# The first modulation by chunks of channels, folded and used chunk by chunk

## The chip, the cores and the metric

The kernel runs on one core of one Trainium2 chip. The metric is the device time of one execution in microseconds (us), as the median of the runs.

## The reference, cut to what matters

Two layers of a first block (two mixers, each with a feed-forward part) and two layers of a second block (attention over a memory, a mixture of experts at the end) act on 256 tokens of `x` and 256 tokens of a context, 1024 channels each. What the change touches is the beginning of layer 0:

```python
mod = silu(c) @ ada_w[0] + ada_b[0]        # 6 x 1024 values; the same with c_ctx for the context
shift, scale = mod[0:1024], mod[1024:2048]  # of the mixer; the other four parts are used later
h  = rmsnorm(x, norm_mix_w[0]) * (1.0 + scale) + shift
hc = rmsnorm(ctx, norm_mix_w[0]) * (1.0 + scale_ctx) + shift_ctx
p  = h @ ab_w_in[0]                         # 1024 -> 2560 columns; hc likewise
```

Apart from this, and at the same time in the kernel, stand the keys and values of the memory of layer 0 (`mem @ xa_w_k`, `mem @ xa_w_v`), which do not depend on `x`.

## The kernel before, in words

Everything is transposed: a tensor of 512 tokens (256 of `x`, side 0; 256 of the context, side 1) lies as 8 chunks of 128 channels on the partitions, with the tokens in the free dimension. Weights come as one long stream of slots of 1 MB (16 tiles of 128x128 f32) through a ring of six slots (`ring`). SyncE issues the loads in order. A load of slot n waits until TensorE has begun slot n-5 (the semaphore `slots_used`). GpSimd's queue issues the other loads.

Large products are done in three: a weight slot is split into a rounded high part (ScalarE, `slot_high_act`, L986) and the rest (VectorE, `slot_low_dve`, L994), the input likewise, and TensorE adds high x high, high x low and low x high in a bank of PSUM. A slot's low part overwrites the slot in the ring. The order of each engine's work is written out by hand; engines meet only through semaphores.

The start of the kernel runs like this on TensorE (L1899 to L1952):

- filler matmuls, then two column groups of the memory's keys with slot K0a, in plain f32
- the first modulation, 2048 columns (`ada_products`, L1909): eight slots A0 to A7, one for each 128 rows of `ada_w`. The weights of the array are the two columns of `silu(c)`, the slot is streamed, and four column groups of the array write 512 columns each, to partitions 0-1, 32-33, 64-65, 96-97 of one bank. Sums over all 1024 rows, so no value is known before A7.
- between them the other keys (K0b), the sums of squares of the norm (L572), the values (V0a, V0b, `mem_value_products`, L1845 to L1849) and the spread of 1/rms over the partitions (L605)
- `turn_rows` (L1937): ScalarE and VectorE copy the four rows of 512 to `ada_row`, TensorE turns them with 16 small matmuls into 16 columns of 128 channels, VectorE adds the bias (L3023) and makes the scale of all 8 chunks (L2968)
- `split_products` (L1182) of the input, `ab_w_in`, slots AB0 and AB1: a pair of output tiles chunk by chunk (L1158 to L1164) as VectorE scales (`rms_split_dve`, L1073), ScalarE shifts and rounds (L1060), and VectorE makes the low part (L1080); then two more output tiles (L1176 to L1180)
- `split_token_products` with AB2 and AB3 (L1222 to L1226), and so on.

VectorE's own order behind the modulation is (L3030 to L3037): the low part of AB0, all chunks of the input, the low part of AB1, then for n = 2 to 6 three chunks of the later modulation (`first_chunks`, L2988, two passes of 128x1024 each) and the low part of slot AB n. The later modulation's chunks wait for the two rows of `silu(c)`, which ScalarE makes from a load (`silu_rows`, L2616); GpSimd issues that load when TensorE has begun AB0 (L3681).

The load order was: memory, K0a, A0, A1, K0b, `x`, `ctx`, A2, A3, V0a, A4, A5, V0b, A6, A7, AB0, AB1, and on.

Of the kernel before, what the change touches and what calls it, by code (L numbers as in the profile page):

```python
# [9 lines left out]
F32 = mybir.dt.float32  # L10
# [3 lines left out]
ALU = mybir.AluOpType  # L14
# [30 lines left out]
    ("ident", P), ("ones", P), ("eps", 2), ("final_norm_w", DC), ("ln_g", 6 * DC), ("ln_b", 6 * DC), ("ckv_gain", 1), ("decay_b", 4), ("head_norm_w", 1),  # L45
# [5 lines left out]
    ("slot_id", P), ("earlier", P), ("fold", 32),  # L51
# [14 lines left out]
SLOTS_ADA = 16 * DC // TILES  # L66
# [10 lines left out]
START = ["K0a", "A0", "A1", "K0b", "A2", "A3", "V0a", "A4", "A5", "V0b", "A6", "A7"]  # L77
# [35 lines left out]
def build(nc, stream, ada_stream, mem_w, c_rows, small, x_t, ctx_t, mem_t, ab_bias, sgu, t5_bias, band_bias, cmp_bias, out):  # L113
    with ExitStack() as ctx:
# [22 lines left out]
        silu_c = sb("silu_c", 2 * DC)  # L137
# [50 lines left out]
        ada_row = area(0, 2048)  # L188
# [1618 lines left out]
        def _(pe):  # L1807
# [98 lines left out]
            sums, ada_bank = bk.next_bank(), bk.next_bank()  # L1906
            rows_out = bk.freed(bk.turn - 1)

            def ada_products(k):  # L1909
                rows, first = w.tiles(TILES)  # L1910
                for j in range(4):
                    m = nc.tensor.matmul(PS[ada_bank][32 * j:32 * j + 2, :], silu_c[:, 2 * k:2 * k + 2],
                                         rows[:, j * 512:(j + 1) * 512], start=k == 0, stop=k == DC - 1)
                    if first and j == 0:
                        m.then_inc(sem("slots_used"), 1)
                if k == DC - 1:
                    m.then_inc(full(ada_bank), 1)

            for k in range(2):
                ada_products(k)  # L1920
            pe.wait_ge(sem("mem_split"), DC)
            mem_key_products(range(2, 4))
            ada_products(2)
# [4 lines left out]
            ada_products(3)  # L1928
            mem_value_products()
            rstd_pe(bk, TT)  # L1930
            for k in range(4, 6):
                ada_products(k)
            mem_value_products()
            for k in range(6, DC):
                ada_products(k)

            def turn_rows():  # L1937
                b = bk.next_bank()
                pe.wait_ge(*rows_out)
                pe.wait_ge(sem("rows_copied"), 1)  # L1940
                for n in range(TILES):
                    columns, rows = PS[b][:, 2 * n:2 * n + 2], ada_row[0:2, n * P:(n + 1) * P]
                    if n == 0:
                        nc.tensor.matmul(columns, rows, ident[0:2, 0:2], start=True, stop=True)
                    else:
                        m = nc.tensor.transpose(columns, rows, ident[0:2, 0:2])
                m.then_inc(full(b), 1)

            turn_rows()
            split_products(bk, w, 4, ab_high, h_part, TT, ab_slot_high, sides=2)  # L1950
# [630 lines left out]
        def _(act):  # L2581
# [14 lines left out]
            nc.scalar.activation(silu_c[:, :], small_at("c2"), ACT.Silu).then_inc(sem("silu_c_ready"), 1)  # L2596
# [3 lines left out]
            slot_high_act(bk, START.index("K0b"), mem_slot_high, fresh=True)  # L2600
# [3 lines left out]
            for name in ("V0a", "V0b"):  # L2604
                slot_high_act(bk, START.index(name), mem_slot_high, fresh=True)
            b = bk.next_bank()
            act.wait_ge(full(b), bk.filled())
            for j in range(2):
                m = nc.scalar.activation(ada_row[0:2, j * 512:(j + 1) * 512], PS[b][32 * j:32 * j + 2, :], ACT.Copy)
            m.then_inc(free(b), 1)  # L2610
            bk.turn += 2
            last = bk.freed(bk.turn - 2)
            for n in range(4):
                bk.fill(MEM_BANKS[n % 2])

# [4 lines left out]
            slot_high_act(bk, AB_AT, ab_slot_high, fresh=True)  # L2620
            slot_high_act(bk, AB_AT + 1, ab_slot_high, fresh=True)
            act.wait_ge(sem("mod_ready"), 1)
            shift_high_act(bk, 0, 0, 2, ab_high, last)
            for t in range(2):
                b = bk.fill(MEM_BANKS[t])
                act.wait_ge(full(b), bk.filled())
                nc.scalar.activation(mem_made_values(t), PS[b][:, :], ACT.Copy).then_inc(free(b), 1)
# [45 lines left out]
            act.wait_ge(sem("mod_ready"), 2)  # L2673
# [17 lines left out]
            act.wait_ge(sem("mod_ready"), 4)  # L2691
# [262 lines left out]
        def _(dve):  # L2954
# [10 lines left out]
            def mod_scaled(l, m, sides=2):  # L2965
                nw = small_at(("norm_mix_w", "norm_ffn_w")[m], "p (l c s) -> p l c s", l=2, c=DC)
                at = slice(24 * m + 8, 24 * m + 16)
                nc.vector.scalar_tensor_tensor(scalev[:, l, m, :, 0:sides], modv[:, l, at, 0:sides], 1.0,  # L2968
                                               nw[:, l, :, 0:sides], ALU.add, ALU.mult).then_inc(sem("mod_ready"), 1)
                dve.wait_ge(sem("mod_ready"), 2 * l + m + 1)  # L2970
# [39 lines left out]
            for c in range(1, 4):  # L3010
                mem_key_out(c)
            root_dve(bk, TT)
            for name in ("V0a", "V0b"):
                slot_low_dve(bk, START.index(name), mem_slot_high)
            b = bk.next_bank()
            dve.wait_ge(full(b), bk.filled())
            for j in range(2, 4):
                ins = nc.vector.tensor_copy(ada_row[0:2, j * 512:(j + 1) * 512], PS[b][32 * j:32 * j + 2, :])
            ins.then_inc(sem("rows_copied"), 1)
            spread = spread_dve(bk)  # L3020
            b = bk.next_bank()
            dve.wait_ge(full(b), bk.filled())
            nc.vector.tensor_tensor(mod[:, 0:32], PS[b][:, 0:32], ada_b[:, 0:32], ALU.add).then_inc(free(b), 1)  # L3023
            dve.wait_ge(*bk.freed(bk.turn - 1))
            for b in MEM_BANKS:
                bk.fill(b)
            marks["mem_out"] = [bk.freed(bk.turn - n) for n in (2, 1)]
            mod_scaled(0, 0)
            dve.wait_ge(sem("x_landed"), 32)
            slot_low_dve(bk, AB_AT, ab_slot_high)  # L3030
            rms_split_dve(bk, 0, 0, 2, ab_high, spread=spread)
            slot_low_dve(bk, AB_AT + 1, ab_slot_high)
# [644 lines left out]
        def _(pool):  # L3677
            pool.dma_start(consts[:, 0:N_EARLY], small[:, 0:N_EARLY]).then_inc(sem("small_landed"), 16)
            nc.gpsimd.memset(filler[:, :], 1.0).then_inc(sem("filler_set"), 1)
# [89 lines left out]
        def _(sp):  # L3769
# [12 lines left out]
            for n in range(4):  # L3782
# [3 lines left out]
            for n in range(4, RING):  # L3786
                load(n)
            before = N_SLOTS - SLOTS_MOE
            groups = before // RING
            with nc.sync.Fori(0, groups - 1) as i:  # L3790
                for n in range(RING, 2 * RING):
                    load(n, i, RING, at=n + i * RING)
# [145 lines left out]
def _layout(i):  # L3938
# [12 lines left out]
    slots_of("A", _by_row(i["ada_w"][0][:, 0:2048]), "01234567")  # L3951
# [64 lines left out]
    arrays = [stream.reshape(N_SLOTS, P, SLOT), ada, mem_w, c_rows, _small(i), turned(i["x"][0]), turned(i["ctx"][0]),  # L4016
# [21 lines left out]
```

## Time and profile before

| what | us |
|---|---|
| median of 3 runs (2561.82 to 2563.05) | 2561.86 |
| profiled execution, whole | 2562.03 |
| its span | 2560.2 |
| TensorE busy | 2497.3 (98%) |
| VectorE busy | 1988.4 (78%) |
| ScalarE busy | 1175.9 (46%) |

The profile is one execution. Times in its rows are counted from the start of the span. In the names of engines PE is TensorE (PEld its weight loads), DVE VectorE, ACT ScalarE, POOL GpSimd, SP SyncE. An f32 matmul stands as two records, one of rounded values as one.

### The profile page before, as it was taken

How to read it: one execution, taken by the hardware profiler on the slowest of the kernel's cores; microseconds unless marked ns; L12 is line 12 of the kernel's file. 1: busy time of each engine (PE TensorE's matmuls, PEld its weight loads, DVE VectorE, ACT ScalarE, POOL GpSimd, SP SyncE). 2: the span in 40 equal slices, each digit the busy share in tenths (PEclk: the TensorE clock that was granted, in tenths of full speed). 3: DMA queues.
4: the chain of work that ended last, by engine and by line, in shares of the span. 5: the costliest groups of instructions: out<-in, count | busy, mean ns of one | idle time of the engine just before them, and what ended most of it. 6: DMA issues, size and time to landing. Idle time of an engine off the chain costs nothing.

```text
span 2560.2 us, 42423 instructions
## 1 busy us (share of the span) xinstructions
PE 2497.3 (98%) x16691; PEld 2147.3 (84%) x16691; DVE 1988.4 (78%) x2455; ACT 1175.9 (46%) x1498; POOL 89.1 (3%) x116
## 2 busy tenths in 40 slices
PE   7999999999999999999999899999999999999998
PEld 5877788888889998889999688888888888888886
DVE  3886877777766886857887748888888888988887
ACT  3435200001421004531014736777777777777776
POOL 0100100000000001000002000000000000000000
PEclk8999999999999999999999999999999999999999
DMA  8843444443335553334555035999899989999996
GB/s 333 315 166 130 168 171 166 168 167 116 116 108 212 186 182 137 111 108 159 185 182 185 15 116 194 373 363 375 334 374 366 363 343 374 366 351 358 362 375 247
DMA packets 91399, 602.77 MB, mean 235 GB/s; under 512 B 9840, under 2 KB 12912, under 8 KB 24688
## 3 DMA queue, kind: packets, MB, share of 16 engines
q1 hardware_dynamic: 76848, 540.05, 55.9%
q0 software_dynamic: 14400, 60.56, 6.7%
q8 instruction: 113, 1.85, 0.3%
q14 instruction: 38, 0.31, 0.0%
HBM read 598.47 MB, written 2.10 MB: 235 GB/s over the span
## 4 chain that ended last, share of the span: by engine, by line
PE 92%; DVE 5%; ACT 2%; issue 1%; DMA 1%; SPq 0%; DVEq 0%; ACTq 0%
PE bank L1176 12%; PE bank L1179 12%; PE bank L1180 12%; PE bank L2477 8%; PE bank L2481 8%; PE bank L2480 8%; PE bank L2508 4%; PE bank L2512 4%; PE bank L2511 4%; PE bank L532 2%; PE bank L1413 1%; PE bank L1434 1%; ACT arena L1458 1%; PE bank L2490 1%; PE bank L572 1%; PE bank L1226 1%
## 5 line engine op out<-in xcount | busy, mean ns | idle before, releaser
L972 DVE TENSOR_TENSOR ring_part<-ring,arena_part 128x2048 fp32r<-128x2048 f32 x481 | 1079.3, 2274 | 29.0 <-ACT arena_part L991 14.6
L2833 ACT ACTIVATE arena_part<-ring 128x2048 fp32r<-128x2048 f32 x339 | 647.6, 1920 | 192.9 <-DMA ring<-in_stream 192.4
L1176 PE MATMUL bank<-arena_part 128*128 128x256 f32 (+1 forms) x2040 | 651.5, 319 | 8.1 <-DVE ring_part L972 8.1
L1180 PE MATMUL bank<-arena_part,ring_part 128*128 128x256 f32 (+1 forms) x2040 | 648.0, 318 | 0.0
L1179 PE MATMUL bank<-h_part,arena_part 128*128 128x256 f32 (+1 forms) x1496 | 474.9, 317 | 0.0
L1176 PEld LDWEIGHTS bank<-arena_part 128*128 128x128 f32 x2040 | 389.9, 191 | 38.7 <-issue 12.4
L1180 PEld LDWEIGHTS bank<-arena_part,ring_part 128*128 128x128 f32 x2040 | 389.9, 191 | 25.7
L2477 PE MATMUL bank<-arena_part,h_part 128*128 128x512 f32 x896 | 354.2, 395 | 0.0
L2481 PE MATMUL bank<-arena_part,h_part 128*128 128x512 f32 x896 | 349.6, 390 | 0.0
L2480 PE MATMUL bank<-ring_part,h_part 128*128 128x512 f32 x896 | 348.9, 389 | 0.0
L1280 ACT ACTIVATE arena<-bank 128x256 f32<-128x256 f32 (+1 forms) x66 | 30.1, 456 | 636.6 <-PE bank L1180 635.6
L1179 PEld LDWEIGHTS bank<-h_part,arena_part 128*128 128x128 f32 x1496 | 285.7, 191 | 18.6
L968 DVE CAST arena_part<-ring 128x2048 fp32r<-128x2048 f32 x115 | 140.5, 1222 | 74.9 <-PE bank L1176 71.0
L2481 PEld LDWEIGHTS bank<-arena_part,h_part 128*128 128x128 f32 x896 | 168.1, 188 | 36.2
L2480 PEld LDWEIGHTS bank<-ring_part,h_part 128*128 128x128 f32 x896 | 168.4, 188 | 33.6
L2477 PEld LDWEIGHTS bank<-arena_part,h_part 128*128 128x128 f32 x896 | 168.3, 188 | 33.2
L2508 PE MATMUL bank<-arena_part 128*128 128x512 f32 x448 | 175.2, 391 | 0.0
L2512 PE MATMUL bank<-arena_part 128*128 128x512 f32 x448 | 174.4, 389 | 0.0
L2511 PE MATMUL bank<-ring_part,arena_part 128*128 128x512 f32 x448 | 174.4, 389 | 0.0
L1179 PE MATMUL bank<-arena_part 128*128 128x256 f32 (+1 forms) x544 | 173.2, 318 | 0.0
L972 DVE TENSOR_TENSOR arena_part<-bank,arena_part 128x512 fp32r<-128x512 f32 x56 | 38.7, 691 | 94.9 <-ACT arena_part L2918 94.9
L1179 PEld LDWEIGHTS bank<-arena_part 128*128 128x128 f32 x544 | 104.3, 192 | 6.8
(376 smaller groups left out, 3087.8 us busy)
## 6 DMA issues: line engine op xcount, KB each, us to landing
ring<-in_stream SPq DMA_DIRECT2D x511, 1024.0 KB, 4.9
arena<-in_ada_stream POOLq DMA_DIRECT2D x80, 512.0 KB, 4.3
consts<-in_mem_w POOLq DMA_DIRECT2D x8, 512.0 KB, 4.0
consts<-in_small POOLq DMA_DIRECT2D x1, 2800.0 KB, 11.6
arena<-in_c_rows POOLq DMA_DIRECT2D x2, 1024.0 KB, 7.6
arena<-in_ab_bias POOLq DMA_DIRECT2D x1, 2048.0 KB, 8.8
arena<-in_t_bias POOLq DMA_DIRECT2D x1, 2048.0 KB, 9.0
arena<-in_mem_t SPq DMA_DIRECT2D x1, 1024.0 KB, 4.9
```

The lines of the kernel that those rows point to most:

```text
L968: nc.vector.tensor_copy(high, value).then_inc(sem("rounded"), 1)
L972: return nc.vector.tensor_tensor(low, value, high.bitcast(F32), ALU.subtract)
L1176: m = nc.tensor.matmul(out_ap, w_high, high, start=start, stop=False)
L1179: nc.tensor.matmul(out_ap, w_high, low, start=False, stop=False)
L1180: return nc.tensor.matmul(out_ap, w_low, high, start=False, stop=stop)
L2477: m = nc.tensor.matmul(PS[b][:, :], x_e_high[:, k, of(e)], high, start=k == 0, stop=False)
L2480: nc.tensor.matmul(PS[b][:, :], x_e_high[:, k, of(e)], low, start=False, stop=False)
L2481: m = nc.tensor.matmul(PS[b][:, :], x_e_low[:, k, of(e)], high, start=False, stop=k == DC - 1)
L2508: m = nc.tensor.matmul(PS[b][:, :], h_high, high, start=f_blk == 0 and f == 0, stop=False)
L2511: nc.tensor.matmul(PS[b][:, :], h_high, low, start=False, stop=False)
L2512: m = nc.tensor.matmul(PS[b][:, :], h_low, high, start=False, stop=f_blk == MB - 1 and f == FB - 1)
L2833: nc.scalar.activation(high, ring[:, where], ACT.Copy).then_inc(sem("moe_high"), 1)
```

## The change

- The weights of the first modulation leave the stream and become a tensor of their own, `ada_mix`: eight pieces of 1 MB, piece c holding all 1024 rows of the 128 shift columns and the 128 scale columns of channel chunk c. They are loaded into the first four rooms of the ring, behind AB1, and the stream goes on behind them.
- `silu_c` becomes eight blocks of 32 columns, two of `silu` and 30 of zero (cleared by GpSimd). For a chunk, column group g takes the rows k = g and then k = 4 + g: eight f32 matmuls of 256 columns, into 4 x 32 partitions of one bank. ScalarE copies the bank to `ada_rows`.
- `fold_rows`: two f32 matmuls with 128x128 of `ada_rows` as weights and the first two columns of `fold` (1 where the partition modulo 32 is the column) sum the four groups and turn the rows. VectorE adds the bias and makes the scale of that chunk alone.
- `first_products`: the products of chunk k with four output tiles at once (slots AB0 and AB1), 12 matmuls of 512 columns, where there were two tiles and then two.
- The loop: products of piece c+2, fold of c+1, products of the input with chunk c.
- Moved: the values of the memory stand earlier and together; the copies of the values out of PSUM, on ScalarE both before, are one on ScalarE and one on VectorE and stand ahead of the modulation; V0b is split by VectorE alone; AB0 and AB1 are split ahead of the modulation.

```diff
-START = ["K0a", "A0", "A1", "K0b", "A2", "A3", "V0a", "A4", "A5", "V0b", "A6", "A7"]
+START = ["K0a", "K0b", "V0a", "V0b"]
@@ tensor
             pe.wait_ge(sem("mem_split"), DC)
             mem_key_products(range(2, 4))
-            ada_products(2)
+            mem_value_products()
+            sums = bk.next_bank()
             for c in range(DC):
                 pe.wait_ge(sem("squared"), bk.up("squared"))
                 m = group_sums(sums, sqv[:, c, :], TT, c == 0, c == DC - 1)
             m.then_inc(full(sums), 1)
-            ada_products(3)
             mem_value_products()
+            marks["values_full"] = [(full(b), bk.filled_in[b]) for b in MEM_BANKS]
             rstd_pe(bk, TT)
...
+            def ada_products(c):
+                b = bk.fill(ADA_BANKS[c % 2])
+                rows_copied.append(bk.freed(bk.turn - 1))
+                pe.wait_ge(free(b), bk.emptied())
+                pe.wait_ge(sem(f"ada_landed{c % ADA_ROOMS}"), 16 * (c // ADA_ROOMS + 1))
+                room = ring[:, c % ADA_ROOMS * SLOT:(c % ADA_ROOMS + 1) * SLOT]
+                for late in range(2):
+                    for g in range(4):
+                        k = 4 * late + g
+                        m = nc.tensor.matmul(PS[b][32 * g:32 * g + 32, X2], silu_c[:, k, :],
+                                             room[:, k * SEQ:(k + 1) * SEQ], start=not late, stop=bool(late))
                 m.then_inc(full(b), 1)
+                ada_made.append((full(b), bk.filled()))
+
+            def fold_rows(c):
+                pe.wait_ge(*rows_copied[c])
+                b = bk.fill(FOLD_BANK)
+                pe.wait_ge(free(b), bk.emptied())
+                for n in range(2):
+                    m = nc.tensor.matmul(PS[b][:, 4 * c + 2 * n:4 * c + 2 * n + 2], ada_rows[c % 4][:, n * P:(n + 1) * P],
+                                         small_at("fold")[:, 0:2], start=True, stop=True)
+                m.then_inc(full(b), 1)
...
+            ada_products(0)
+            ada_products(1)
+            fold_rows(0)
+            for c in range(DC):
+                if c + 2 < DC:
+                    ada_products(c + 2)
+                if c + 1 < DC:
+                    fold_rows(c + 1)
+                first_products(c)
+            w.t += 2 * TILES
@@ scalar
+            copy_rows(0)
+            copy_rows(1)
+            for c in range(DC):
+                if c + 2 < DC:
+                    copy_rows(c + 2)
+                for s in range(2):
+                    t = slice(SEQ * s, SEQ * (s + 1))
+                    scaled_act(bk, c == DC - 1 and s == 1, spread_last)
+                    nc.scalar.activation(ab_high[:, c, t], hv[:, c, t], ACT.Identity, bias=shift(0, 0, c, s))\
+                        .then_inc(sem("in_high"), 1)
@@ vector
+            for c in range(DC + 1):
+                if c < DC:
+                    b = bk.fill(FOLD_BANK)
+                    dve.wait_ge(full(b), bk.filled())
+                    both = modv[:, 0, c:c + DC + 1:DC, :]
+                    nc.vector.tensor_tensor(both, PS[b][:, 4 * c:4 * c + 4].rearrange("p (n s) -> p n s", n=2),
...
+                    nc.vector.scalar_tensor_tensor(scalev[:, 0, 0, c, :], modv[:, 0, DC + c, :], 1.0, mod_w[:, 0, c, :],
+                                                   ALU.add, ALU.mult).then_inc(sem("dve_step"), 1)
+                    dve.wait_ge(sem("dve_step"), bk.up("dve_step"))
+                    for s in range(2):
+                        t = slice(SEQ * s, SEQ * (s + 1))
+                        ins = nc.vector.scalar_tensor_tensor(hv[:, c, t], xv[:, c, t], scalev[:, 0, 0, c, s:s + 1],
+                                                             PS[spread][:, t], ALU.mult, ALU.mult)
+                        scaled_dve(ins, c == DC - 1 and s == 1, spread)
+                if c:
+                    for s in range(2):
+                        t = slice(SEQ * s, SEQ * (s + 1))
+                        dve.wait_ge(sem("in_high"), bk.up("in_high"))
+                        ins = nc.vector.scalar_tensor_tensor(h_part[:, c - 1, t], hv[:, c - 1, t], shift(0, 0, c - 1, s),
+                                                             ab_high[:, c - 1, t].bitcast(F32), ALU.add, ALU.subtract)
+                    ins.then_inc(sem("in_split"), 1)
             bk.turn += 4 + 4
             dve.wait_ge(sem("c_rows_ready"), 1)
@@ sync
+            for j in range(DC):
+                if j >= ADA_ROOMS:
+                    sp.wait_ge(*marks["ada_made"][j - ADA_ROOMS])
+                elif j == ADA_ROOMS - 1:
+                    for made in marks["values_full"]:
+                        sp.wait_ge(*made)
+                else:
+                    sp.wait_ge(sem("slots_used"), j + 2)
+                room = ring[:, j % ADA_ROOMS * SLOT:(j % ADA_ROOMS + 1) * SLOT]
+                sp.dma_start(room, ada_mix[j, :, :]).then_inc(sem(f"ada_landed{j % ADA_ROOMS}"), 16)
```

The new load order is: memory, K0a, K0b, `x`, `ctx`, V0a, V0b, AB0, AB1, the eight pieces, AB2, and on.

## Rows read from the trace of the kernel before

**Rows 1.** The page's busy times: us, share of the span, instructions.
```profile
PE 2497.3 (98%) x16691; PEld 2147.3 (84%) x16691; DVE 1988.4 (78%) x2455; ACT 1175.9 (46%) x1498; POOL 89.1 (3%) x116
```

**Rows 2.** The chain of waits, 0 to 260: start us, us, what.
```profile
30.08 1.79 PE bank L572 x64
...
57.12 0.94 PE bank L1946 x15
58.59 2.29 DVE ring_part L972
...
71.90 1.34 DVE h_part L1080 x4
...
75.83 0.47 PE bank L1176
```

**Rows 3.** Windows: stretch, length; busy us and records of each engine; clock, DMA share, GB/s.
```profile
125.00:130.00 5.00, 5.00 (x24) 4.14 (x23) 4.96 (x8) 0.60 (x1) 1.05 (x2) 1.00 0.58 202
```

**Rows 4.** Timeline of TensorE: start us, us, engine, line, what.
```profile
86.81 0.39 PE L1222 MATMUL bank<-arena_part 128*128 128x512 f32 x1
...
141.20 0.39 PE L1176 MATMUL bank<-arena_part 128*128 128x512 f32 x1
141.43 0.39 PE L1179 MATMUL bank<-h_part,arena_part 128*128 128x512 f32 x1
```

**Rows 5.** Timeline of VectorE, 69 to 140; in brackets the idle time before.
```profile
69.46 0.86 DVE L1073 SCALAR_TENSOR_TENSOR h_normed<-x_stream,mod_scale,bank 128x256 f32<-128x256 f32 x2
70.25 0.87 DVE L1080 SCALAR_TENSOR_TENSOR h_part<-h_normed,mod,arena_part 128x256 fp32r<-128x256 f32 x2
...
76.83 1.23 DVE L2983 SCALAR_TENSOR_TENSOR arena<-arena 128x1024 f32<-128x1024 f32 x1 [1.14 <-ACT arena L2618]
...
83.71 2.29 DVE L972 TENSOR_TENSOR ring_part<-ring,arena_part 128x2048 fp32r<-128x2048 f32 x1
...
138.00 2.28 DVE L972 TENSOR_TENSOR ring_part<-ring,arena_part 128x2048 fp32r<-128x2048 f32 x1
```

**Rows 6.** Timeline of all engines, 0 to 40.
```profile
10.01 7.14 PE L1824 MATMUL bank<-arena,ring 128*128 128x256 f32 x32
...
17.08 1.90 PE L1912 MATMUL bank<-ring,silu_c 128*2 128x512 f32 x16
17.39 1.91 ACT L991 ACTIVATE arena_part<-ring 128x2048 fp32r<-128x2048 f32 x1 [4.88 <-DMA ring<-in_stream]
...
22.73 0.20 ACT L637 ACTIVATE stats<-consts 128x1 f32<-128x1 f32 x1 [2.13 <-DMA x_stream<-in_ctx_t]
...
36.53 0.77 PE L1845 MATMUL bank<-arena_part 128*128 128x512 f32 x1 [3.84 <-DVE ring_part L972]
```

**Rows 7.** The page's groups: count, busy us, mean ns of one, idle before.
```profile
L1280 ACT ACTIVATE arena<-bank 128x256 f32<-128x256 f32 (+1 forms) x66 | 30.1, 456 | 636.6 <-PE bank L1180 635.6
...
L968 DVE CAST arena_part<-ring 128x2048 fp32r<-128x2048 f32 x115 | 140.5, 1222 | 74.9 <-PE bank L1176 71.0
```

**Rows 8.** Timeline of ScalarE, 69 to 77.
```profile
69.97 0.91 ACT L1060 ACTIVATE arena_part<-h_normed,mod 128x256 fp32r<-128x256 f32 x2 [0.67 <-DVE h_normed L1073]
...
73.59 1.28 ACT L2618 ACT_TABLE_LOAD   x1
74.88 1.92 ACT L2618 ACTIVATE arena<-arena 128x2048 f32<-128x2048 f32 x1
```

**Rows 9.** The page's loads: queue, count, KB each, median us to landing.
```profile
ring<-in_stream SPq DMA_DIRECT2D x511, 1024.0 KB, 4.9
```

**Rows 10.** Windows of 0.5 us where TensorE begins again and where its clock rises.
```profile
36.50:37.00 0.50, 0.47 (x1) 0.50 (x2) 0.00 (x0) 0.00 (x0) 0.00 (x0) 0.50 1.03 426
41.50:42.00 0.50, 0.50 (x3) 0.41 (x2) 0.50 (x1) 0.00 (x0) 0.00 (x0) 0.53 0.53 213
62.50:63.00 0.50, 0.46 (x1) 0.49 (x2) 0.50 (x2) 0.50 (x2) 0.00 (x0) 0.50 0.00 0
65.50:66.00 0.50, 0.50 (x3) 0.37 (x3) 0.50 (x3) 0.50 (x2) 0.21 (x1) 0.63 1.02 426
```

More of the change, by code:

```diff
@@ L50 @@
     ("sinks", 8), ("expert_id", EXPERTS), ("cmp_row_ok", 2),
-    ("slot_id", P), ("earlier", P), ("fold", 32),
+    ("slot_id", P), ("earlier", P),
 ]
@@ L110, in leave, with build @@
         self.i = None
-def build(nc, stream, ada_stream, mem_w, c_rows, small, x_t, ctx_t, mem_t, ab_bias, sgu, t5_bias, band_bias, cmp_bias, out):
+def build(nc, stream, ada_mix, ada_stream, mem_w, c_rows, small, x_t, ctx_t, mem_t, ab_bias, sgu, t5_bias, band_bias, cmp_bias, out):
     with ExitStack() as ctx:
@@ L1904, in _ @@
             pe.wait_ge(sem("silu_c_ready"), 1)
[L1906 to L1920, printed above, removed]
             pe.wait_ge(sem("mem_split"), DC)
             mem_key_products(range(2, 4))
-            ada_products(2)
+            mem_value_products()
+            sums = bk.next_bank()
             for c in range(DC):
@@ L2599, in _ @@
                 nc.scalar.activation(mem_high[:, c, :], mem_in[:, c, :], ACT.Copy).then_inc(sem("mem_rounded"), 1)
-            slot_high_act(bk, START.index("K0b"), mem_slot_high, fresh=True)
+            for name in ("K0b", "V0a"):
+                slot_high_act(bk, START.index(name), mem_slot_high, fresh=True)
             act.wait_ge(sem("x_landed"), 32)
@@ L2603, in _, with copy_rows @@
             root_act(bk, TT, 0)
[L2604 to L2612, printed above, removed]
+            for n in range(2):
+                slot_high_act(bk, AB_AT + n, ab_slot_high, fresh=True)
             for n in range(4):
                 bk.fill(MEM_BANKS[n % 2])
+            b = bk.fill(MEM_BANKS[0])
+            act.wait_ge(full(b), bk.filled())
+            nc.scalar.activation(mem_made_values(0), PS[b][:, :], ACT.Copy).then_inc(free(b), 1)
+            bk.fill(MEM_BANKS[1])
+            bk.turn += 1
+            spread_last = bk.freed(bk.turn - 1)
+            def copy_rows(c):
+                b = bk.fill(ADA_BANKS[c % 2])
+                act.wait_ge(full(b), bk.filled())
+                nc.scalar.activation(ada_rows[c % 4], PS[b][:, X2], ACT.Copy).then_inc(free(b), 1)
+            copy_rows(0)
[8 more added lines that the diff above has]
+                        .then_inc(sem("in_high"), 1)
+            for _ in range(DC):
+                bk.fill(FOLD_BANK)
             def silu_rows(rows, times):
@@ L3009, in _ @@
             slot_low_dve(bk, START.index("K0b"), mem_slot_high)
-            for c in range(1, 4):
-                mem_key_out(c)
+            mem_key_out(1)
+            mem_key_out(2)
+            slot_low_dve(bk, START.index("V0a"), mem_slot_high)
+            mem_key_out(3)
+            split_slot(bk, START.index("V0b"), None, highs=mem_slot_high)
             root_dve(bk, TT)
-            for name in ("V0a", "V0b"):
-                slot_low_dve(bk, START.index(name), mem_slot_high)
-            b = bk.next_bank()
+            for n in range(2):
+                slot_low_dve(bk, AB_AT + n, ab_slot_high)
@@ L3789, in _ @@
             groups = before // RING
-            with nc.sync.Fori(0, groups - 1) as i:
-                for n in range(RING, 2 * RING):
+            with nc.sync.Fori(0, groups - 2) as i:
+                for n in range(2 * RING, 3 * RING):
                     load(n, i, RING, at=n + i * RING)
```

112 lines of the change are left out of this document (60 added, 52 removed).

## The prediction

> **What bounds the kernel now.** I read the shares of busy time first: TensorE is busy 98% of the span, the other engines are not near it [rows 1]. So a microsecond counts only where TensorE stands still, and the change touches only the first 90 us. The chain of waits shows the place: TensorE ends the columns of the modulation at 58.06, VectorE spends 2.29 us on the first input slot, then scales and splits chunk after chunk until 73.24 and splits the second slot right behind, and TensorE goes on at 75.83 [rows 2]. From there it has no hole: a stretch of 5 us holds 5.00 us of it [rows 3], and the values' products begin at 86.81 [rows 4]. These need slot AB2 in two parts, and VectorE ends that at 83.71 + 2.29 = 86.00, only 0.8 us earlier, because three chunks of the later modulation stand before it (six passes, from 76.83 on) [rows 5]. The same order, three chunks and then a slot, repeats for later slots: AB7 is split at 138.00 + 2.28 = 140.28 [rows 5] and needed at 141.20 [rows 4]. The reader is to see two queues that run side by side with next to no play: **what counts is not when TensorE gets its first product, but when VectorE is through with the modulation and reaches AB2.** A change that frees TensorE earlier and VectorE later loses.
>
> **Start, up to the first product.** Eight MB of modulation weights leave the front of the load queue. The fifth 1 MB transfer of it landed at 17.4 and the seventh at 22.7 [rows 6], so 2.65 us each. In the new order K0b is third (12.1), V0a sixth (20.0), V0b seventh (22.7), AB0 and AB1 by 28, the modulation's chunks 0 and 1 by 33.4.
> - K0a's products run from 10.01 to 17.15 as before [rows 6]. K0b is split by then, its 48 matmuls of 256 columns, half of the 0.23 us that 512 take [rows 4], run 17.3 to 23.0.
> - V0a: ScalarE 1.91 us [rows 6] from 20.0, VectorE 2.29 us, the fourth key copy some 0.4 us (ScalarE's of that size is 0.46 [rows 7]): TensorE starts 24.8, 24 matmuls at 0.23 us [rows 4] end 30.3.
> - Sums 1.8 us [rows 2]: 32.2. V0b was split by VectorE meanwhile (1.22 [rows 7] and 2.29 us): products 32.3 to 37.8. Spread, half as many records as the sums, 0.9 us: 38.9.
> - Modulation products: 16 records took 1.90 us for 2 MB [rows 6]; a chunk now is 1 MB in eight matmuls of 256 columns, four column groups side by side: 0.95 us. Chunk 0 ends 39.95, chunk 1 41.0.
> - The fold is two f32 matmuls with 128x128 weights and two columns, four records; the trace has none like it. Below: the turns at 0.94/15 = 0.06 us a record [rows 2], 0.25 us. Above: K0a's records at 7.14/32 = 0.22 us [rows 6], 0.9 us. I take 0.45, since two columns stream next to nothing and only the weights count. Fold 0 ends 41.55, chunk 2's products 42.6.
> - ScalarE is in order: it copies chunk c+2's rows before it shifts chunk c. Copy 0.46 us [rows 7], two shifts 0.91 us [rows 8], about 0.1 us for handing over: 1.5 us. **First product of the input at 44.1**, where the kernel now has its first in the half microsecond from 62.50 [rows 10]: 18 us won, and spent in the loop.
>
> The Trainium skill, in "TensorE: Matmul & The Clock Gate", Part 3 (Packing small matmuls), gives 2.38 times for three column tiles side by side. Worked out as an estimate for four, that is 3.17 times and 1.13 us instead of 0.95 for a chunk, 1.1 us more over the six chunks inside the loop, and 2566.4 in the end. The trace disagrees: eight matmuls of 512 columns in 1.90 us are 0.24 us each, against 0.89 us for one alone (twice 7.14/16), so 3.75 times [rows 6].
>
> **The loop.** Per chunk TensorE does 12 matmuls (240 lie between 86.81 and 141.20 [rows 4], 0.227 us each: 2.72 us), 0.95 us for chunk c+2, 0.1 us between. The fold hides beside ScalarE's copy. But products of chunk c wait for both shifts, these wait behind the copy of chunk c+2, and that one waits for products made just before: 1.5 us in which TensorE has only the fold. Period 1.5 + 2.72 + 0.1 + 0.95 = 5.27 us. VectorE needs 0.53 us from the fold's end through bias and scale (58.06 to 58.59 [rows 2]), 0.79 for two scalings (69.46 to 70.25) and as much for two splits [rows 5], 2.1 us: never the limit. Loads: chunk j waits for chunk j-4's products, three periods ahead, against 4.9 us to land [rows 9]: hidden. Chunk 5's products start at 44.1 + 5 x 5.27 = 70.45 and end 73.2; fold 7 ends 73.75. VectorE then has bias and scale, two scalings, split 6 and split 7, 0.53 + 3 x 0.79: **it is through at 76.6**. TensorE, limited by split 6, ends the four tiles at 79.5 (before: 86.8).
>
> **After the loop.** VectorE's next work are the three chunks, which wait for the activated rows. ScalarE ends the last shift at about 75.5; table load 1.28 and the pass 1.92 us [rows 8] make 78.7. The rows themselves are in time: GpSimd issues their load at TensorE's first product of the input, 31 us before. First pass at 78.8, **2.0 us later than 76.83**. The value copies that left ScalarE's queue (1.1 us) are in this already. AB2 is split at 88.0, so TensorE, idle from 79.5, begins the values' products at 88.1: 1.3 us late. The copies and slot splits moved into the start stand beside TensorE's 5.5 us stretches; if they were uncovered they would cost up to 2 us before 44.1, and as much in the end.
>
> **The clock.** After 8.6 us of nothing TensorE starts at the lower level. The trace shows this twice: work began at 36.5 with a granted clock of 0.50, and it stayed there until about 41.6; work began at 62.5 and it stayed until about 65.7 [rows 10]. So 5.1 and 3.2 us at 1.2 GHz instead of 2.4, a loss of 2.6 and 1.6 us. In this kernel the second one fell where VectorE was the limit and cost little; in the new one it falls on the values' products, with TensorE the limit from there. I take 2.1 us. Price with its bounds: 1.6 to 2.6.
>
> Sum: +1.3 + 2.1 = +3.4 us. VectorE is then 2.0 us late and TensorE 3.4, so no later slot is waited for; both keep the distance to the end. The profiled execution took 2562.03 (span 2560.2 and 1.8 around it), which gives 2565.4; it lies 0.2 above the median of the runs, so **2565.3**.
>
> **Rivals.** A measurement of this kernel tells about 0.2%, 5.1 us, from no change.
> - A, the loop is paced by TensorE alone (period 4.3, copy and shift hidden better than I think): five periods of 1.0 us less, VectorE is through at 71.8, products of AB2 start at 83.3, -3.5 + 2.1: 2560.5. For it: the shifts of chunk c could start in the period before. Against: ScalarE's order. 0.22.
> - B, TensorE's lead is kept and values' products start at 79.5: -7.3, 2554.6. Against: six passes at 1.15 us stand between the last split and AB2's, whatever TensorE does. 0.05 for this or anything as large.
> - C, other side: TensorE, with 1.1 us holes in each period and a pause of 1.8 us before V0a, falls to the lower level inside the loop. A period then is 1.5 + 5.4 + 0.1 + 1.9 = 8.9, so 3.6 us more each; one is enough to leave the 0.2% (2568.9), two give 2572.5, seven 2590. For: it was at the lower level at 36.5 after one pause only [rows 10]. Against: that pause was 3.8 us with no work in it (until 36.53 [rows 6]), and 80% of each period is work. 0.08.
> - D, each hand-over costs 0.1 us more than I took (five in a period, seven periods): 3.5 us on the end of VectorE's part, 2568.8. 0.10.
> - The forecast, 2562.5 to 2567: 0.55.
>
> Both ends of the fold's price (it is on the path twice) give -0.4 and +0.9. Range 2559.5 to 2569: it holds the forecast, A and most of D, and leaves out B and C. Faster by over 0.2%: B and a little of A, 0.06. Slower: C and D and the upper end of the forecast, 0.18. The same: 0.76.
>
> **What would show it.** In the timeline: first product of the input near 44 (right if 42 to 47); starts of chunk c's products 5.3 us apart, each after a shift of ScalarE; the first later chunk on VectorE near 79; TensorE idle for 7 to 9 us before the values' products, ended by VectorE's split of AB2; a granted clock of 0.5 in the 3 to 5 us after it. The forecast is wrong if the period is under 4.5 or over 6, if AB2's split ends before 85, or if the clock is at 0.5 between 45 and 79.

## The result and the profile after

The changed kernel takes 2567.16 us (median of 22 runs, 2562.46 to 2569.06). The kernel before takes 2561.86 on the same chip (22 runs, 2559.03 to 2563.83). The ratio is 1.0018, 95% interval [1.0012, 1.0024]: 3.1 to 6.1 us slower, a little on the slow side of "no difference", with the edge of 5.1 us inside the interval. The forecast was 2565.3, in a range up to 2569. The profiled execution of the changed kernel took 2563.34 (span 2561.5), which lies near the fast end of its runs; why, is told below.

The page's busy times answer to [rows 1]:

```profile
PE 2495.5 (97%) x16770; PEld 2146.4 (84%) x16770; DVE 1992.0 (78%) x2469; ACT 1174.0 (46%) x1502; POOL 89.3 (3%) x117
```

Everything that the change does lies in the first 90 us. The chain of waits of the changed kernel, from 0 to 130 (start us, us, what), answers to [rows 2]:

```profile
25.11 0.47 PE bank L1845
...
30.95 1.88 PE bank L572 x64
32.83 0.43 PE bank L1845
...
39.59 1.73 PE bank L1934 x32
41.32 0.54 PE bank L1944 x4
41.86 1.04 PE bank L1934 x16
42.93 0.38 ACT arena L2650
43.31 0.80 ACT arena_part L2660 x2
44.16 0.50 PE bank L1958
46.27 0.91 PE bank L1966 x4
47.17 1.05 PE bank L1934 x16
48.24 0.38 ACT arena L2650
48.62 0.80 ACT arena_part L2660 x2
49.47 0.50 PE bank L1958
...
70.75 0.50 PE bank L1958
...
75.99 1.28 ACT L2667
77.29 1.93 ACT arena L2667
79.24 1.23 DVE arena L3024 x2
...
86.20 2.22 DVE ring_part L972
88.55 0.76 PE bank L1222
```

One turn of the loop can be read off it. TensorE makes a piece's products (L1934), ScalarE copies them (L2650) and only then shifts the chunk of two pieces earlier (L2660), and TensorE's products of the input (L1958) wait for that. From 44.16 to 49.47 is 5.31 us, and it is the same five times, up to 70.75. Then the chain leaves TensorE: ScalarE's table and pass, the three later chunks on VectorE, the split of AB2 (L972), and last the values' products (L1222) at 88.55, where they stood at 86.81 before [rows 4].

The same place in TensorE's timeline (in brackets the idle time before, and what ended it):

```profile
25.11 0.47 PE L1845 MATMUL bank<-arena_part 128*128 128x512 f32 x1 [2.05 <-DVE arena L3043]
...
79.12 1.07 PE L1966 MATMUL bank<-h_part,arena_part 128*128 128x512 f32 x4
88.55 0.76 PE L1222 MATMUL bank<-arena_part 128*128 128x512 f32 x1 [8.36 <-DVE ring_part L972]
89.11 0.63 PE L1225 MATMUL bank<-ring_part,arena_part 128*128 128x512 f32 x1
```

So TensorE is free 6.6 us earlier (80.2 against 86.8), stands still for 8.36 us, and begins 1.74 us later. Then it is slow: starts are 0.43 us apart, where 0.23 is usual [rows 4]. Windows of the changed kernel show the clock (stretch, length, busy us and records of PE, PEld, DVE, ACT, POOL, then PE's granted clock, DMA share, GB/s); the last is for later on:

```profile
82.50:83.00 0.50, 0.00 (x0) 0.00 (x0) 0.50 (x3) 0.50 (x1) 0.00 (x0) 0.77 1.24 524
83.00:83.50 0.50, 0.00 (x0) 0.00 (x0) 0.50 (x1) 0.50 (x2) 0.00 (x0) 0.50 0.70 287
88.50:89.00 0.50, 0.45 (x1) 0.48 (x2) 0.50 (x1) 0.00 (x0) 0.00 (x0) 0.50 0.95 377
92.50:93.00 0.50, 0.50 (x3) 0.37 (x2) 0.50 (x3) 0.00 (x0) 0.00 (x0) 0.50 0.97 410
93.00:93.50 0.50, 0.50 (x4) 0.41 (x3) 0.50 (x1) 0.00 (x0) 0.22 (x1) 0.99 1.00 393
1400.00:1440.00 40.00, 34.31 (x270) 27.26 (x271) 31.81 (x90) 23.52 (x66) 9.16 (x2) 1.00 0.15 55
```

The clock fell to half (1.2 GHz) in the pause and came back at 93.0, after 4.5 us of work. At the full clock that work takes half of this time, so the fall costs 2.2 us.

Where the rest of the kernel stands is read from a mark that both have, ScalarE's table load ahead of the second mixer. In the kernel before, then in the changed one:

```profile
312.94 1.28 ACT L1280 ACT_TABLE_LOAD   x1
```

```profile
317.09 1.28 ACT L1280 ACT_TABLE_LOAD   x1
```

That is 4.15 us, and as much at 617.64 and 621.79: 1.74 + 2.2 and some tenths. But at the end of the kernel the two profiled executions are only 1.3 us apart. Table loads of ScalarE that both have show where they come together. At 1089.51 and 1092.25 they are 2.74 apart. TensorE of the kernel before has a wait shortly ahead of that which the changed one doesn't have:

```profile
1041.39 2.00 PE L1413 MATMUL bank<-arena 64*128 64x256 f32 x16 [1.20 <-ACT arena L2587]
```

All profiles with the new start lack this wait and gain about 1.5 us on before there; b1, which has the old start, has the wait and gains nothing. So it goes with the change, but why is not shown. At 1396.19 and 1399.69 the two are 3.50 apart again, and at 1483.04 and 1484.16 only 1.12. This last step has to do with the clock: from 1400 to 1440 that of the execution before was

```profile
1400.00:1440.00 40.00, 36.22 (x258) 27.29 (x257) 31.82 (x91) 23.53 (x67) 9.16 (x2) 0.87 0.15 53
```

0.87, with a fall to 0.50 from about 1414 to 1424, and the changed kernel's was 1.00. Nothing there was changed, and all the other profiles of this document have a fall at that place. Four of the changed kernel's 22 runs have a mean clock of 0.996 or more, as the profiled one has, and take 2562.5 to 2564.3; the other 18 have 0.993 or 0.994 and take 2564.9 to 2569.1. **The profiled execution is one of the few with a fall less**, so the medians, not the two spans, tell the cost. e10 below is in all but one load the changed kernel, and its profile has the fall at 1414 and one more at the start: its span is 5.7 us above before's (2565.9 against 2560.2), which is near the 5.3 of the medians.

### The profile page after: what moved, and what is told of

It reads as the page before. It is cut to its first block, busy times and chain, and to the rows that moved or that the text cites. A ratio compares the mean times of both kernels' runs of the same rounds, so it can differ in the third digit from the quotient of the medians.

```text
span 2561.5 us, 42582 instructions
## 1 busy us (share of the span) xinstructions
PE 2495.5 (97%) x16770; PEld 2146.4 (84%) x16770; DVE 1992.0 (78%) x2469; ACT 1174.0 (46%) x1502; POOL 89.3 (3%) x117
## 4 chain that ended last, share of the span: by engine, by line
PE 91%; DVE 4%; ACT 2%; issue 1%; DMA 1%; SPq 0%; DVEq 0%; ACTq 0%
PE bank L1176 12%; PE bank L1179 12%; PE bank L1180 12%; PE bank L2506 8%; PE bank L2510 8%; PE bank L2509 8%; PE bank L2537 4%; PE bank L2541 4%; PE bank L2540 4%; PE bank L532 2%; PE bank L1413 1%; PE bank L1434 1%; PE bank L572 1%; ACT arena L1458 1%; PE bank L1222 1%; PE bank L2519 1%
## 5 line engine op out<-in xcount | busy, mean ns | idle before, releaser
L972 DVE TENSOR_TENSOR ring_part<-ring,arena_part 128x2048 fp32r<-128x2048 f32 x481 | 1079.5, 2274 | 24.1 <-ACT arena_part L2874 9.9
L1180 PE MATMUL bank<-arena_part,ring_part 128*128 128x256 f32 (+1 forms) x2024 | 641.2, 317 | 0.0
L1179 PE MATMUL bank<-h_part,arena_part 128*128 128x256 f32 (+1 forms) x1480 | 468.6, 317 | 0.0
L972 DVE TENSOR_TENSOR arena_part<-bank,arena_part 128x512 fp32r<-128x512 f32 x56 | 38.7, 691 | 93.6 <-ACT arena_part L2959 93.6
## 6 DMA issues: line engine op xcount, KB each, us to landing
consts<-in_small POOLq DMA_DIRECT2D x1, 2784.0 KB, 11.3
```

The costliest lines, as they stand in the source:

```text
L972: return nc.vector.tensor_tensor(low, value, high.bitcast(F32), ALU.subtract)
L1179: nc.tensor.matmul(out_ap, w_high, low, start=False, stop=False)
L1180: return nc.tensor.matmul(out_ap, w_low, high, start=False, stop=stop)
```

## The experiments

Each was timed in five rounds beside the kernel before, in three groups with a median of before of their own (2562.35 for e1 to e4, 2561.78 for e5 to e8, 2561.89 for b1, e9 and e10). e6 and e8 have 5 runs each, the others 10 or 11, the changed kernel 22. The changed kernel was not timed again in them, so a difference from its 2567.16 goes across groups. Medians, and the ratio to before:

| kernel | median us | ratio, 95% |
|---|---|---|
| changed | 2567.16 | 1.0018 [1.0012, 1.0024] |
| e1, AB2 split first | 2567.36 | 1.0019 [1.0009, 1.0028] |
| e2, and sgu's weights early | 2555.87 | 0.9976 [0.9967, 0.9985] |
| e3, shift before copy | 2563.95 | 1.0008 [0.9999, 1.0017] |
| e4, fillers in the pause | 2562.03 | 1.0002 [0.9993, 1.0011] |
| e5, e2 and late constants early | 2555.59 | 0.9976 [0.9967, 0.9985] |
| e6, e5 with e3, AB2 in the loop | 2551.72 | 0.9961 [0.9948, 0.9975] |
| e7, fillers ahead of V0a | 2564.24 | 1.0009 [1.0000, 1.0018] |
| e8, e6 with e7 | 2549.48 | 0.9956 [0.9942, 0.9970] |
| b1, e2's order in the kernel before | 2561.88 | 0.9999 [0.9990, 1.0008] |
| e9, e4 with e7 | 2561.78 | 1.0000 [0.9991, 1.0009] |
| e10, sgu's weights early alone | 2566.39 | 1.0016 [1.0007, 1.0025] |

### AB2 ahead of the three chunks: e1, e2, b1, e10

```diff
+        ab_slot_high[AB_AT + 2] = part_area(8192, SLOT)     # a room of its own
@@ scalar, behind the last shift
+            slot_high_act(bk, AB_AT + 2, ab_slot_high, fresh=True)
@@ vector, behind the loop
+            slot_low_dve(bk, AB_AT + 2, ab_slot_high)
-            for n in range(2, 7):
-                first_chunks(3 * n - 6, 3 * n - 3)
+            for n in range(3, 7):
+                first_chunks(3 * n - 9, 3 * n - 6)
```

The diff is cut: ScalarE's old rounding of AB2 is gone from its place, and each later group of chunks stands one slot later, to the end of the 24.

> The changed kernel with one thing moved: slot AB2 gets a room of its own for its high part (it no longer waits for AB0's), ScalarE rounds it right behind the last shift and VectorE makes its low part before the first three chunks of the later modulation; every later slot has the chunks one group later. My theory (the values' products wait for VectorE's order, not for the modulation): TensorE starts them at about 80.3 instead of 88.55 and stays at the full clock, so that stage is 8.3 + 2.3 us earlier. But the weights of the gate (sgu) are loaded only when the 24th chunk of the later modulation is used, and that stays where it was (load issued near 159, landed near 164), while TensorE now gets to the gate's products near 156.5: a new pause of 7 to 8 us there, perhaps with a cold start behind it. Whole time 1 to 5 us below the changed kernel, near the kernel before. Rival (only the order ahead of AB2 counts): no pause at the gate, 10 us below the changed kernel, 2556 to 2557. Rival (the modulation itself is the limit): values' products still at 86 or later, no change.

Nothing was won: 2567.36, where 1 to 5 us had been expected. The pause at 80 is gone (the values' products begin at 81.65, within 0.1 us of the four tiles), and TensorE is then ahead of before. It gives it all back at the gate. Timelines of TensorE and of VectorE in e1:

```profile
167.04 5.62 PE L1995 MATMUL bank<-arena 128*128 128x128 f32 x32 [8.95 <-DMA arena<-in_sgu]
```

```profile
128.19 1.22 DVE L3024 SCALAR_TENSOR_TENSOR arena<-arena 128x1024 f32<-128x1024 f32 x1 [4.76 <-DMA arena<-in_ada_stream]
```

TensorE came to the gate at 158.1 and found the gate's weights (sgu) not there; they land at 167.0, when the kernel before had begun the gate at 162.97. The pause had been expected, 7 to 8 us long; it took 8.95. The clock fell in it, until 172, and once in the loop (44 to 48). GpSimd issues that load only when VectorE has used all chunks, and e1 put the chunks later. A wait that nothing in the trace before shows, since its load was in time there, took the place of the one removed. e2 takes it away:

```diff
                 if k == 12:
                     pool.dma_start(consts[:, N_EARLY:], small[:, N_EARLY:]).then_inc(sem("sgu_landed"), 16)
+                    pool.wait_ge(sem("slots_used"), AB_AT + 4)
+                    pool.dma_start(area(8192, 1024), sgu).then_inc(sem("sgu_landed"), 16)
             pool.wait_ge(sem("chunk_used"), len(ADA_FIRST))
-            pool.dma_start(area(AB_BIAS + 4096, 1024), sgu).then_inc(sem("sgu_landed"), 16)
```

> As e1_ab2_first, and the gate's weights are loaded to a place that is free from slot AB3 on, beside the 13th chunk. My theory: values' products at about 80.3, the gate's at about 156.5 without a pause, attention about 6.5 us earlier than in the kernel before, whole time near 2555.5, 6 us below the kernel before and 10 to 11 below the changed one. If it is no better than e1_ab2_first, the gate's weights were not what held TensorE there.

2555.87, 11.3 us below the changed kernel and 6.5 below the one before. The mark of 312.94 stands in e2 at

```profile
308.06 1.28 ACT L1281 ACT_TABLE_LOAD   x1
```

which is 4.9 us ahead of before. The clock stays up from 40 to 200 too. Two controls say what of this belongs to what. b1 makes all of e2's edits in the kernel before; e10 makes sgu's load early in the changed kernel and nothing else.

> The kernel before, with only what e2 added to the new one: slot AB2 gets a room of its own, ScalarE rounds it right behind its last shift, VectorE splits it before the first three late chunks (each later chunk then stands one group later), and sgu's weights come beside the 13th chunk. Nothing of the new modulation is in it. In the trace before, TensorE ends the four tiles at 86.8 and AB2 is split at 86.0, so TensorE has no idle time there to win. If the order pays only together with the new modulation (which frees TensorE 7 us before AB2): no change, within 1 us of before (2562). If what e2 gained is the order's and sgu's own gain, whatever stands ahead: 6 us below before, 2556.

> The new kernel with sgu's weights loaded to a free room beside the 13th chunk, and nothing else of e2. In the new kernel the gate's products start with slack behind that load (TensorE is 4 us later there than before), so if e2's gain over e1 was only the removal of a wait that e1's order had brought, nothing changes: 2567, within 1 us. If the early load also helps by itself (another load that stands behind it in the queue, or a clock fall near 160 to 171 less): 2 to 5 us below the new kernel.

b1: 2561.88 against 2561.89, nothing. Its values' products begin at 86.25, as soon as TensorE is through with the tiles; the order has no idle time to win. e10: 2566.39, within 1 us of the changed kernel. Both came as expected. So the gain of e2 is neither the order's nor the load's alone: it is the 6.6 us by which the new modulation frees TensorE, once AB2 and sgu's weights stop holding it. **The change had a gain, and it was lost at VectorE's queue behind the loop.**

### The loop: e3

```diff
             for c in range(DC):
-                if c + 2 < DC:
-                    copy_rows(c + 2)
                 for s in range(2):
                     ...                    # the two shifts of chunk c
+                if c + 2 < DC:
+                    copy_rows(c + 2)
```

> The changed kernel with one thing changed: in the loop ScalarE shifts chunk c before it copies the rows of chunk c+2. My theory (the period is products of c+2, copy, shifts, products of c in a row): the period falls from 5.3 to about 4.7 us, where VectorE's bias, scale, scalings and split of the chunk before end last; VectorE is through near 73.6 instead of 77.0, values' products start near 85 instead of 88.55, the lower clock behind the pause stays. Whole time 3 to 3.5 us below the changed kernel. Rival (TensorE or the loads set the period): period unchanged, no change. Rival A of the forecast (TensorE alone, period 4.3): 5 us below.

2563.95, 3.2 us below the changed kernel, as expected. Its loop is no longer ended by the shift. In TensorE's timeline of e3 the products wait for VectorE's part only, and shortly:

```profile
45.42 0.50 PE L1958 MATMUL bank<-arena_part 128*128 128x512 f32 x1 [0.47 <-ACT arena_part L2658]
...
52.13 1.19 PE L1966 MATMUL bank<-h_part,arena_part 128*128 128x512 f32 x4 [0.19 <-DVE h_part L3091]
...
57.02 1.19 PE L1966 MATMUL bank<-h_part,arena_part 128*128 128x512 f32 x4 [0.18 <-DVE h_part L3091]
...
61.90 1.21 PE L1966 MATMUL bank<-h_part,arena_part 128*128 128x512 f32 x4 [0.18 <-DVE h_part L3091]
```

The period is 4.9 us instead of 5.3, though not the 4.7 that was expected, and TensorE has little idle time left in it: from 48 to 60 it is busy for 11.63 us, where it was 9.84 in the changed kernel.

```profile
48.00:60.00 12.00, 11.63 (x88) 7.17 (x88) 4.16 (x14) 2.98 (x7) 0.87 (x2) 1.00 1.01 422
```

In that profile the values' products begin at 87.68, only 0.87 us before the changed kernel's 88.55, and not near 85 as expected, because V0a's products ran at the lower clock (the next point). Against e10, which has this fall too and the changed kernel's loop, e3 needs 2.4 us less from V0a's first product to the values' first (62.56 against 64.96). The 3.2 us of the medians are more than that, by less than their intervals.

### The clock: e4, e7, e9

```diff
             def warm_spare(b, n):      # in both kernels: n matmuls of 256 columns into a free bank; they feed nothing
                 pe.wait_ge(free(b), bk.filled_in[b])
                 for _ in range(n):
                     nc.tensor.matmul(PS[b][:, X2], filler[:, 0:P], filler[:, :], start=True, stop=True)
@@ e4: ahead of split_token_products with AB2
+            warm_spare(bk._turn(bk.turn)[0], 62)
@@ e7: ahead of the first mem_value_products (V0a)
+            warm_spare(0, 15)
@@ e9: both
```

> The changed kernel with 62 bf16 matmuls of 256 columns (about 7.8 us) put into TensorE's pause between the four tiles and the values' products; they feed nothing. Theory (the price of the lower clock is half of the time at 1.2 GHz behind the pause): values' products still start near 88.5, but at 2.4 GHz: 2.3 us below the changed kernel, about 2564.9. Rival (the clock there costs nothing because VectorE is the limit of the next slots): no change. Rival (the fillers come to stand in the way): later start, slower.

> The changed kernel with 15 bf16 matmuls (1.9 us) in TensorE's 2.0 us pause before V0a's products. Theory (the changed kernel is 4.0 us late in its profile and 5.3 in the median because in most executions the clock falls in this pause and V0a's products run at 1.2 GHz for about 3 us): V0a's products always at the full clock, 1 to 1.5 us below the changed kernel in the median. Rival (the spread comes from later pauses alone): same as the changed kernel, and the profile no different from its.

> The new kernel with both sets of filler products, 15 ahead of V0a and 62 in the pause behind the four tiles, nothing else changed; they feed nothing. If the two clock prices are separate (each filler alone took 3 to 5 us off the median), they add up only as far as neither alone took the other's part: 2.3 us for the pause at 80 to 88 (read from the profile's records) and 1.5 to 2.5 for the pause at 23 to 25: 2562 to 2563, and what is left against before is the late split, +1.7 us less the clock falls that come later. If each filler also takes away falls much later in the kernel, as the e4 profile suggested: below 2561, faster than before. If one of them already removes all there is to win: 2564.

e4: 2562.03, 5.1 us below the changed kernel (4.1 by the two ratios), twice what was expected. e7: 2564.24, 2.9 below, where 1 to 1.5 was expected. e9: 2561.78, 5.4 below. So e4's fillers were worth more than the clock at 83 to 93 explains in one profile, e7's more than the 1.5 us that the fall at V0a costs (below; the intervals leave room for both differences), and the two together little more than e4's alone; the intervals of e4 and e9 (each about 2.3 us to either side) overlap. What they do is seen in the timeline of e9:

```profile
80.16 6.94 PE L1897 MATMUL bank<-filler 128*128 128x256 bf16 x62
88.68 0.47 PE L1222 MATMUL bank<-arena_part 128*128 128x512 f32 x1 [1.57 <-DVE ring_part L972]
...
89.45 0.40 PE L1222 MATMUL bank<-arena_part 128*128 128x512 f32 x1
```

The values' products still begin at 88.68, but at once with 0.23 us from one to the next. The mark of 312.94 stands at 314.93: 2.0 us late instead of 4.15. That isolates the late split, +1.9 us, from the clock, 2.2 us. In the profiles with a pause there and no fillers (changed, e3, e7, e10) the clock fell each time; with fillers (e4, e9) never.

The second price is that of the pause ahead of V0a, 2.05 us long. In the profiled execution of the changed kernel the clock stayed up there. In e3, e4, e5, e6 and e10, which have the same start, it fell. A window of e3, then one of the changed kernel:

```profile
25.00:28.00 3.00, 2.88 (x7) 2.36 (x8) 2.97 (x3) 3.00 (x6) 0.00 (x0) 0.54 1.03 434
```

```profile
25.00:28.00 3.00, 2.89 (x13) 2.38 (x14) 2.97 (x3) 3.00 (x6) 0.00 (x0) 1.00 1.01 426
```

Seven records where thirteen stood. What it costs is the same each time. From V0a's first product to the spread of 1/rms (L605) TensorE needs 13.4 us in the six profiles without this fall (changed, e1, e2, e7, e8, e9: in the changed kernel 25.11 to 38.51) and 14.9 in the five with it (in e3 25.12 to 40.07): 1.5 us, and the whole loop is later by as much. In e10, which has both falls and is otherwise the changed kernel up to there (sgu's early load aside), the mark of 312.94 stands at

```profile
318.90 1.28 ACT L1280 ACT_TABLE_LOAD   x1
```

6.0 us after before and 1.8 after the changed kernel's profile; its execution had a span of 2565.9. In e1 the clock fell from 44 to 48 instead. So with that start and no fillers it fell in six of eight profiles, once inside the loop; with fillers (e7, e8, e9), in none of three. Three profiles alone would be few, since it stayed up at V0a in three of the eight too.

### The rest of the chain: e5, e6, e8

e5 is e2 with the load of the late constants issued behind the third chunk, where it was behind the 13th. e6 adds e3's order, and rounds and splits AB2 inside the loop:

```diff
@@ scalar, in the loop
+                if c == 4:
+                    slot_high_act(bk, AB_AT + 2, ab_slot_high, fresh=True)
@@ vector, in the loop
+                if c == 5:
+                    slot_low_dve(bk, AB_AT + 2, ab_slot_high)
```

e8 is e6 with e7's 15 fillers.

> e2_ab2_first_sgu with the load of the late constants (2.8 MB), which stood beside the 13th chunk of the later modulation and held VectorE 13 to 15 us there, issued right behind the first three chunks, near 46 us. Theory: VectorE's waits for chunks 13 and 14 shrink to a few us, the 0.5 us for which TensorE waited there goes, nothing else moves, since TensorE is fed: within 1 us of e2_ab2_first_sgu. Rival (VectorE was the limit there): 3 us or more less. Rival (the load takes the bandwidth of the modulation's pieces): period of the loop over 5.3, slower.

> e5_small_early, and ScalarE shifts before it copies (as e3_shift_first), and slot AB2 is rounded and split inside the loop, where ScalarE and VectorE stand idle for 2 to 3 us of each period. Theory: period 4.9, four tiles done near 76.5, values' products follow at once (80.2 before), all later work 3 to 4 us earlier than in e5_small_early: about 2552. If VectorE's chunks are the limit behind AB2, TensorE waits for AB3 near 87 and the gain is under 2 us.

> e6_in_loop with the fillers of e7_warm_v0a: 1 to 1.5 us below e6_in_loop if the clock falls there in most executions, the same otherwise.

e5: 2555.59, no change beside e2, as expected. VectorE's waits for the later chunks' loads fell from 6.3 us in e2 (5.94 at 128.08 and 0.40 at 130.86, less than half of the 13 to 15 that the expectation names) to 0.65, and TensorE gained nothing by it. e6: 2551.72, as expected (2552). e8: 2549.48, 2.2 below e6 where 1 to 1.5 was expected; medians of five runs each can't tell the two apart. In e8 TensorE runs from the loop into the values' products without a pause:

```profile
76.79 1.07 PE L1968 MATMUL bank<-h_part,arena_part 128*128 128x512 f32 x4
77.69 0.39 PE L1223 MATMUL bank<-arena_part 128*128 128x512 f32 x1
```

and the mark stands at

```profile
303.85 1.28 ACT L1281 ACT_TABLE_LOAD   x1
```

9.1 us ahead of before. This version beats both kernels: 0.9956 [0.9942, 0.9970] of before, 11 us by the ratio and 12 by the medians.

## Why the prediction was right, and where it was off

- **What bounds.** Right. "What counts is when VectorE is through and reaches AB2" is the result in one sentence, and e2 with b1 shows it from both sides: the same earlier TensorE is worth 6.5 us when AB2 doesn't hold it, and AB2's new place alone is worth nothing.
- **Start.** V0a at 25.11 (24.8), sums ended 32.8 (32.2), one piece 0.96 us each for the first two (0.95; one piece alone 1.04), first product of the input 44.16 (44.1). The fold took 0.54 us (0.45, bounds 0.25 and 0.9), and the second and third pieces ended 0.3 us later than forecast; ScalarE's copy and shifts with their hand-overs took 1.25 (1.5), and the errors cancel. The estimate that was worked out from the Trainium skill ("TensorE: Matmul & The Clock Gate", Part 3), 1.13 us a piece, lies above what was measured, 0.96 to 1.05.
- **Loop.** Period 5.31 (5.27), each turn ended by ScalarE's shift. The sum is closer than its terms: copy and shifts 1.25 (1.5), the twelve products 3.01 (2.82 with the 0.1 between), the piece 1.05 (0.95). This is in part luck. e3 shows the cause that was given, the copy ahead of the shift. Rival A asked for a period of 4.3, and even e3's, with TensorE busy for 97% of it, is 4.9.
- **After the loop.** First late chunk at 79.24 (78.8), AB2 split 86.12 + 2.29 = 88.4 (88.0), values' products 88.55 (88.1). The term of +1.3 measured +1.74.
- **Clock behind the pause.** 4.5 us of work at the half clock, 2.2 us (forecast 2.1, bounds 1.6 to 2.6). Sum of the stage 4.15 (at the mark of 312.94) against the forecast's 3.4. This profile lacks the fall at V0a; e10, with it, has 5.96.
- **What was missed.** The median is 5.3 above before, 1.9 above the forecast. The size fits the clock's fall at V0a: 1.5 us, in five profiles of eight. Rival C had the place and the direction ("a pause of 1.8 us before V0a") but saw it inside the loop at 3.6 us a period; there it fell once in eight (e1, from 44 to 48), and that turn took 6.92 us, 1.6 more than the others. It got 0.08, and what is true of it belonged into the sum as a term of 0 to 1.5 us. The forecast counted the pauses of the new order and priced only the long one.
- **The way to the end.** "Both keep the distance to the end" is not what the traces show, and here the number was lucky. The 4.15 us of the changed kernel's profile are 2.74 at 1092 and 3.50 at 1400, the 5.96 of e10's are 4.30 and 5.08 there. Without the 1.5 us that come back near 1041, the median would be further off than it is.
- **Rival B** (lead kept, 2554.6) doesn't happen in this kernel, for the reason given. It is about what e2 gets (2555.9). **D** would have shown as a longer period and in the hand-overs. The period was right to 0.04 us, and in its chain the hand-overs are 0.02 to 0.04 us each, so it is out.

"The same" was right by the bound of 5.1 us only as far as its interval reaches: the median lies at that bound, 2567.16 against 2561.86.

Open: e4 and e9 gain 5.1 and 5.4 us against the changed kernel. Counted from e10, which has both falls, the mark of 312.94 shows 2.6 for e4 (318.90 to 316.33) and 4.0 for e9 (to 314.93). The rest, 2.5 and 1.4 us, may lie within the intervals, or it is falls later in the kernel: in e4's profile the one near 650 is missing, which before, changed, e9 and e10 all have, and its distance from before shrinks by 1.6 us there. One profile for each kernel can't settle it.

## What to carry to other kernels

When a change frees the bottleneck engine earlier, look at what the next product needs and walk back each of its inputs, also those whose loads had slack before: here the engine's lead was worth nothing until a split was moved ahead of three chunks, and then nothing again until a load was moved too. On an engine that works in order, put the instruction that somebody waits for ahead of the one that prepares a later turn. And a new pause of TensorE has two prices, its length and the slower work behind it; fill it with products that feed nothing, or close it.

## What the runs showed of the hardware

- Four column groups side by side: a piece's eight matmuls of 256 columns take 0.96 to 1.04 us, 0.12 to 0.13 each. The Trainium skill, in "TensorE: Matmul & The Clock Gate", Part 3 (Measured speedup vs the span model), lists 2.38 times for three column tiles; the traces of this case show more for four: one f32 matmul of 256 columns alone took 0.45 us (7.14/16, [rows 6]), and 0.45 against 0.12 to 0.13 is 3.4 to 3.7 times.
- TensorE's clock fell after a pause of only 2.05 us, and not every time (five of eight profiles); work then ran at 0.5 for some 3 us and took 1.5 us longer. With fifteen fillers, which took 1.81 us, it stayed up in three of three. After the pause of 8.4 us it fell in four of four, and with 62 fillers in none of two.
- A fold of two f32 matmuls with 128x128 weights and two columns took 0.54 us, so 0.13 to 0.14 us a record: between the 0.06 of the small turns and the 0.22 of a record with 256 columns, the two neighbours that the forecast had.
- Falls of the clock elsewhere in the kernel (near 650, 1414 to 1424, and at the end) come and go from one execution to the next, and the one at 1414 to 1424 was worth 2.4 us (the two kernels are 3.50 apart at 1396 and 1.12 at 1483), the one near 650 1.6 (e4 is 3.39 behind before at 618 and 1.75 at 683). That is more than some of the edits here. Two profiles of one kernel can differ by more than the edit that one wants to see; a mark in the middle of the kernel, read beside the clock, tells the stage's own shift.
